# Decode attention's value product one step later than its transposes, in a kernel with merged prompt and decode attention

## The chip, the cores and the metric

The kernel runs on one core of a Trainium2 chip. The metric is the device time of one execution in microseconds (us). The core has five engines that run programs of their own and meet at semaphores: TensorE (PE; its weight loads are listed as PEld), the vector engine (DVE), the scalar engine (ACT), GpSimd (POOL) and SyncE (SP, which here only issues transfers). GpSimd issues transfers too.

## The reference

One inference step of a decoder layer, for a prompt of 1024 tokens and for 8 sequences with 8 new tokens each. Half of the width is gated linear attention, the other half differential attention; output projection, feed-forward and a gated embedding follow. The change is in differential attention, which for the 8 sequences reads a paged cache of 4096 past tokens:

```python
def diff_attend_sample(q, k, v, lam, k_past, v_past):
    ...
    s_past = jnp.einsum('bqhcd,bkhcd->bhcqk', q, k_past).astype(F32) * scale
    s_new = jnp.einsum('bqhcd,bkhcd->bhcqk', q, k).astype(F32) * scale
    s_new = jnp.where(jnp.tril(jnp.ones((T, T), dtype=bool)), s_new, -jnp.inf)
    a = jax.nn.softmax(jnp.concatenate([s_past, s_new], axis=-1), axis=-1)
    w = (a[:, :, 0] - lam * a[:, :, 1]).astype(v.dtype)
    return (jnp.einsum('bhqk,bkhv->bqhv', w[..., :P], v_past)
            + jnp.einsum('bhqk,bkhv->bqhv', w[..., P:], v))
```

A sequence has 32 pages of 128 tokens for the keys and as many for the values, 256 KB a page; 8 sequences make 256 pages of each.

## The kernel before

The kernel is a row of stages. The function `attention` is the third; it works on the prompt's attention and the sequences' attention at once, in one list of `STEPS` = 74 steps, t = 0 to 73, that every engine walks in its own program. The order on each engine is written out by hand; semaphore counts join the engines.

The decode part cuts the cache into groups of 4 pages (512 tokens): `NG` = 8 groups for a sequence, `NKV` = 64 in all. Group t goes through these operations:

- step t: TensorE transposes the keys of the group, one head at a time (`turn_keys`, L1587), into PSUM; ACT copies heads 0 to 2 to SBUF as `dec_kt` (L1470), DVE head 3 (L1751);
- step t + 1: `score` (L1599) multiplies them with the queries;
- step t + 2: DVE takes the maximum (L1756) and copies the scores to `dec_s` (L1762);
- step t + `LAG`, with `LAG` = 9, since the softmax of a sequence needs the maximum over its 8 groups: ACT makes the exponentials (`exps`, L1481), TensorE transposes them (`turn_p`, L1622), DVE copies the transposes to `dec_pt` (`take_p`, L1790, two buffers), and TensorE multiplies them with the values (`values`, L1641), summing a sequence in one PSUM bank.

Once per sequence b there are: `score_new` (L1609) and `take_new` (L1772 to L1778) for the new tokens at t = 8b + 8 and 8b + 9; the exponentials, transpose and copy of their weights (L1486, `turn_new_p` L1616, `take_new_p` L1784) in the step of the sequence's first group (t = 8b + 9); their product with the new values (L1634) ahead of the first value product; `final_scale` (L1796 to L1800); `finalize` (L1807), where DVE scales the finished sum to `dec_osc`; `merge` (L1649), a matmul that adds the two sub-heads; and `copy_os` (L1492) on ACT.

Key transposes, merges, transposed weights and new scores share a ring of three PSUM banks, the class `Ring`. An entry takes the next slot in TensorE's order, and may be filled once the entry three places earlier has been copied out by its owner.

The prompt's units fill the gaps: two steps for a unit, with scores (L1547), exponentials (L1446), their combination (L1728), transposes (L1560), weight copies (L1456), output (L1569) and two output copies (L1462, L1463). The last unit's output stands in step 66. After it DVE normalises the prompt's output in four pieces (`norm_prompt`, L1735).

SyncE loads key pages, GpSimd value pages (L1303). Both rings hold four groups; the loads of value group n wait until the value product of group n - 4 is done:

```python
                else:
                    gp.wait_ge(d["pv_done"], n - VR + 1)
                load_pages(gp, m.table, io["cache_v"], m.vr, n % VR, v_page_in[n % VR], n)
```

After the last load GpSimd scales two tiles of `w_out` (L1428). The next stage begins when all engines have left this one.

Of the kernel before, what the change touches and what calls it, by code (L numbers as in the profile page):

```python
# [1234 lines left out]
NG = NPG // 4  # L1235
NKV = DB * NG
LAG = NG + 1
STEPS = NKV + LAG + 1
UNITS = [(h, i) for h in range(H) for i in (0, 7, 1, 6, 2, 5, 3, 4)]
NU = len(UNITS)  # L1240
HALVES = 2 * NU + 3
# [14 lines left out]
class Ring:  # L1256
# [4 lines left out]
    def __init__(self):  # L1261
        self.index, self.emptied, self.owners = {}, {}, []
        count = {"act": 0, "dve": 0}

        def use(key, owner):
            self.index[key] = len(self.owners)
            count[owner] += 1
            self.emptied[key] = count[owner]
            self.owners.append((owner, count[owner]))

        for t in range(STEPS):
            if t < NKV:
                for h in range(H):
                    use(("keys", t, h), "act" if h < 3 else "dve")
            b, last = divmod(t - LAG - NG, NG)
            if last == 0 and 0 <= b < DB:
                use(("merge", b), "act")
            v = t - LAG
            if 0 <= v < NKV:
                if v % NG == 0:  # L1280
                    use(("new_p", v // NG), "dve")
                use(("p", v), "dve")
            b, last = divmod(t - NG, NG)
            if last == 0 and 0 <= b < DB:
                use(("new_s", b), "dve")
# [33 lines left out]
def attention(nc, io, m, ps, scr, sems):  # L1319
# [57 lines left out]
    with nc.Block() as block:  # L1377
# [53 lines left out]
        @block.scalar  # L1431
        def _(act):
            def prompt_exps(k):

                if not 0 <= k < 2 * NU:
                    return
                n, c = divmod(k, 2)
                i, u = UNITS[n][1], n % 2
                act.wait_ge(s["neg_max"], k + 1)
                if k == 0:  # L1440
                    act.wait_ge(gla_stored, 32)
                    act.wait_ge(d["states_stored"], 32)
                if n >= 2:
                    act.wait_ge(s["turned"], pieces_before(n - 1))
                out = m.ap[:, u, c, 0:2 * shown(i) * P].rearrange("p (b two n) -> p two b n", two=2, n=P)
                act.activation(out, score_view(i).rearrange("p two (b n) -> p two b n", n=P), ACT.Exp, scale=SC,  # L1446
                               bias=neg_p[:, u, c:c + 1], accum_out=sums[:, u, c:c + 1]).then_inc(s["exp_done"], 1)

            def copy_weights(n, q):

                i, u = UNITS[n][1], n % 2
                a, b = 4 * q * P, min(4 * q + 4, i + 1) * P
                act.wait_ge(s["turned"], pieces_before(n) + q + 1)
                if n >= 1:
                    act.wait_ge(s["o_done"], n)
                act.activation(m.wt[:, a:b], W_BANK[:, 0:b - a], ACT.Copy).then_inc(s["wt_copied"], 1)  # L1456

            def copy_out(n):

                (h, i), u = UNITS[n], n % 2  # L1460
                act.wait_ge(s["o_done"], n + 1)
                act.activation(m.a_o[:, i, h * DV:h * DV + DV], W_BANK[:, 0:DV], ACT.Copy, scale=rcp[:, u, 0:1])  # L1462
                act.activation(m.junk[:, :], W_BANK[:, 0:DV], ACT.Square, scale=rcp[:, u, 0:1],  # L1463
                               accum_out=m.a_ss[:, i, h:h + 1]).then_inc(s["o_squared"], 1)

            def take_keys(t, h):
                act.wait_ge(d["ring_filled"], ring.filled(("keys", t, h)))
                if t >= 2:
                    act.wait_ge(d["s_full"], t - 1)
                act.activation(m.kt[:, t % 2, h, :], ring_bank(("keys", t, h)), ACT.Copy).then_inc(d["ring_act"], 1)  # L1470

            def exps(v):
                b, g = divmod(v, NG)
                if g == 0:
                    act.wait_ge(d["negm"], b + 1)
                    if b >= 2:
                        act.wait_ge(d["final"], 4 * (b - 2) + 1)
                act.wait_ge(d["s_taken"], v + 1)
                if v >= 2:
                    act.wait_ge(d["ring_filled"], ring.filled(("p", v - 2)))  # L1480
                act.activation(m.pg[:, v % 2, :], m.ss[:, 512 * g:512 * g + 512], ACT.Exp, scale=SC,  # L1481
                               bias=negm[:, b % 2:b % 2 + 1], accum_out=esum[:, b % 2, g:g + 1]).then_inc(d["exp_done"], 1)
                if g == 0:
                    if b:
                        act.wait_ge(d["ring_filled"], ring.filled(("new_p", b - 1)))
                    act.activation(m.pn[:, 0:NS], m.ss[:, PAST:PAST + NS], ACT.Exp, scale=SC,  # L1486
                                   bias=negm[:, b % 2:b % 2 + 1], accum_out=esum[:, b % 2, NG:NG + 1]
                                   ).then_inc(d["expn_done"], 1)

            def copy_os(b):  # L1490
                act.wait_ge(d["ring_filled"], ring.filled(("merge", b)))
                act.activation(m.os[:, b, :], ring_bank(("merge", b))[0:32, 0:DV], ACT.Copy).then_inc(d["ring_act"], 1)  # L1492

            for t in range(STEPS):
                v = t - LAG
                n, c = divmod(t, 2)
                first_group = 0 <= v < NKV and v % NG == 0
                if 0 <= v < NKV and not first_group:
                    exps(v)
                if t < NKV:  # L1500
                    take_keys(t, 0)
                    take_keys(t, 1)
                if c == 1 and 0 <= n - 1 < NU:
                    copy_weights(n - 1, 0)
                prompt_exps(t - 1)
                if first_group:
                    exps(v)
                if c == 0 and 0 <= n - 2 < NU:
                    copy_out(n - 2)
                if t < NKV:  # L1510
                    take_keys(t, 2)
                if t == 0:
                    act.wait_ge(s["lam_step"], 2)
                    act.activation(m.sc[:, 18:20], m.sc[:, 16:18], ACT.Exp).then_inc(s["lam_step"], 1)
                if c == 1 and 0 <= n - 1 < NU and pieces_of(n - 1) == 2:
                    copy_weights(n - 1, 1)
                if t >= LAG + NG and (t - LAG - NG) % NG == 0:
                    copy_os((t - LAG - NG) // NG)
                if t == HALVES:
                    act.wait_ge(s["o_squared"], NU)  # L1520
                    act.activation(m.a_ss[:, 0:TT - 1, :], m.a_ss[:, 0:TT - 1, :], ACT.Ln, scale=1.0 / DV, bias=m.eps[:, :]
                                   ).then_inc(s["ln_done"], 1)
                    act.wait_ge(s["ln_done"], 1)
                    act.activation(m.a_ss[:, 0:TT - 1, :], m.a_ss[:, 0:TT - 1, :], ACT.Exp, scale=-0.5
                                   ).then_inc(s["rstd_done"], 1)

        @block.tensor
        def _(pe):
# [117 lines left out]
            def merge(b):  # L1646
                pe.wait_ge(d["final"], 4 * b + 4)
                emptied(("merge", b))
                pe.matmul(ring_bank(("merge", b))[0:32, 0:DV], const(m, "merge"), m.osc[:, :], start=True, stop=True  # L1649
                          ).then_inc(d["ring_filled"], 1)  # L1650

            pe.wait_ge(d["zero_done"], 4)
            for t in range(STEPS):
                v = t - LAG
# [8 lines left out]
                if t < NKV:  # L1663
                    turn_keys(t, 2)
                    turn_keys(t, 3)
                if t >= LAG + NG and (t - LAG - NG) % NG == 0:
                    merge((t - LAG - NG) // NG)
                if 0 <= v < NKV:
                    if v % NG == 0:
                        turn_new_p(v // NG)  # L1670
# [5 lines left out]
                    score(t - 1)  # L1676
                if t and t % NG == 0 and t // NG <= DB:
                    score_new(t // NG - 1)
                if 0 <= v < NKV:
                    values(v)  # L1680

        @block.vector
        def _(dve):
# [118 lines left out]
            def finalize(b):  # L1802
                dve.wait_ge(d["final"], b * 4 + 3)
                dve.wait_ge(d["pv_done"], NG * b + NG)
                if b:
                    dve.wait_ge(d["ring_filled"], ring.filled(("merge", b - 1)))
                dve.tensor_scalar(m.osc[:, :], O_BANK[:, 0:DV], cs[:, 1:2], None, ALU.mult).then_inc(d["final"], 1)  # L1807
# [4 lines left out]
            for t in range(STEPS):  # L1812
                v = t - LAG
                n, c = divmod(t, 2)
                if t >= LAG + NG and (t - LAG - NG) % NG == 0:
                    finalize((t - LAG - NG) // NG)
                if 0 <= t - 2 < NKV:
                    max_scores(t - 2)
                if 0 < t - 1 <= NKV and (t - 1) % NG == 0:
# [1325 lines left out]
```

## Time and profile before

| what | value |
|---|---|
| time, median of 3 runs | 1888.35 us (1885.49 to 1888.97) |
| the profiled execution: time, and span in the trace | 1886.4 us, 1884.7 us |
| PE busy in the span | 1775.2 us (94%) |
| DVE, ACT, POOL busy | 1196.6, 736.4, 345.6 us |
| attention stage in the trace | about 432 to 872 us |

Busy time tells what an engine has to do, not that others wait for it. Which of its waits are long, and what ends them, is in the views of waits and in the timeline. A number after a timeline row in brackets is the engine's idle time just ahead of it, and what ended that.

### The profile page before, as it was taken

Reading aid. Unit: us, or ns where it says so; the run is one execution under the profiler, and the core shown is the slowest. Engines: PE = TensorE matmul, PEld = TensorE weight load, DVE = VectorE, ACT = ScalarE, POOL = GpSimd, SP = SyncE. Lnnn points to the kernel's source line nnn. Section 1 sums busy time; section 2 is a strip of 40 time slices with the busy share of each in tenths; the row PEclk is TensorE's granted clock in tenths of the full one; section 3 lists DMA queues with packets and bytes.
Section 4 is the critical chain, followed back from the end, with each engine's and each line's share of the span. In section 5 each row is a group of like instructions: output and inputs, shape, how many; then the busy total and the mean of one; then the engine's idle time right before and its main releaser. Section 6 shows DMA issues by size and latency. Waiting matters only on the chain.

```text
span 1884.7 us, 35480 instructions
## 1 busy us (share of the span) xinstructions
PE 1775.2 (94%) x13062; PEld 1639.1 (87%) x13062; DVE 1196.6 (63%) x1946; ACT 736.4 (39%) x1418; POOL 345.6 (18%) x360
## 2 busy tenths in 40 slices
PE   6999999986999999996999999999999999998998
PEld 6999999984666667665898999999999999998997
DVE  4223642475777777765448877666767888789443
ACT  5113322563556565653224332322232424344420
POOL 1111331001233333332111221121111000000110
PEclk9999999998999999997999999999999999999999
DMA  5323551228999999976011222222222424232121
GB/s 161 107 80 82 141 140 56 72 72 254 323 338 351 349 360 355 351 229 223 28 41 45 92 69 69 80 79 72 69 81 69 157 68 145 74 106 75 57 70 48
DMA packets 232923, 265.73 MB, mean 141 GB/s; under 512 B 16162, under 2 KB 173428, under 8 KB 232756
## 3 DMA queue, kind: packets, MB, share of 16 engines
q1 hardware_dynamic: 211988, 195.36, 33.1%
q0 software_dynamic: 20768, 68.17, 10.6%
q8 instruction: 101, 1.65, 0.4%
q14 instruction: 66, 0.54, 0.1%
HBM read 229.79 MB, written 29.21 MB: 137 GB/s over the span
## 4 chain that ended last, share of the span: by engine, by line
PE 46%; DVE 5%; ACT 1%; issue 1%; DMA 1%; DVEq 0%; ACTq 0%
PE psum L2513 33%; PE psum L150 11%; DVE x_second_lo L2527 1%; DVE unit_lo L1910 1%; DMA x_second_lo_raw<-scratch_z 1%; PE psum L2193 1%; PE psum L2889 0%; ACT unit_hi L1904 0%; DVE rstd_and_products L2571 0%; DVE x_second_lo_raw L2531 0%; DVE h L2571 0%; DVE x_first_lo L2527 0%; ACT x_second_hi L2401 0%; DVE x_lo L2222 0%; DMA x_first_hi_raw<-scratch_z 0%
## 5 line engine op out<-in xcount | busy, mean ns | idle before, releaser
L2513 PE MATMUL psum<-x_second_hi,unit_hi 128*128 128x364 f32 x924 | 304.3, 329 | 8.0 <-DVE x_second_lo L2527 4.8
L2513 PE MATMUL psum<-x_second_lo,unit_hi 128*128 128x364 f32 x924 | 303.1, 328 | 0.0
L2513 PE MATMUL psum<-x_second_hi,unit_lo 128*128 128x364 f32 x924 | 303.1, 328 | 0.0
L1303 POOL DMA_DIRECT2D dec_v<-in_cache_v x256 | 138.0, 539 | 290.3 <-issue 283.8
L150 PE MATMUL psum<-x_hi,w_hi 128*128 128x364 f32 x768 | 182.4, 346 | 9.1 <-DVE x_lo L2222 5.8
L2513 PEld LDWEIGHTS psum<-x_second_hi,unit_hi 128*128 128x128 f32 x924 | 173.7, 188 | 10.9 <-issue 5.6
L2513 PE MATMUL psum<-x_first_hi,unit_hi 128*128 128x364 f32 x528 | 173.7, 329 | 0.4 <-DVE x_first_lo L2527 0.4
L2513 PEld LDWEIGHTS psum<-x_second_hi,unit_lo 128*128 128x128 f32 x924 | 173.7, 188 | 0.0
L2513 PEld LDWEIGHTS psum<-x_second_lo,unit_hi 128*128 128x128 f32 x924 | 173.6, 188 | 0.0
L2513 PE MATMUL psum<-x_first_hi,unit_lo 128*128 128x364 f32 x528 | 173.5, 329 | 0.0
L2513 PE MATMUL psum<-x_first_lo,unit_hi 128*128 128x364 f32 x528 | 173.2, 328 | 0.0
L150 PE MATMUL psum<-x_hi,w_lo 128*128 128x364 f32 x768 | 170.7, 330 | 0.0
L150 PE MATMUL psum<-x_lo,w_hi 128*128 128x364 f32 x768 | 170.0, 330 | 0.0
L1470 ACT ACTIVATE dec_kt<-psum 128x512 f32<-128x512 f32 x192 | 108.7, 599 | 156.1 <-PE psum L1587 156.1
L1904 ACT ACTIVATE unit_hi<-unit_sums 128x512 fp32r<-128x512 f32 (+1 forms) x136 | 83.3, 618 | 217.6 <-PE psum L2513 185.2
L2392 POOL TENSOR_TENSOR w_raw<-w_raw,gains 128x1024 f32<-128x1024 f32 x42 | 90.7, 2160 | 376.2 <-DMA w_raw<-in_w_ffn_gate 208.8
L1587 PE MATMUL psum<-consts,dec_k 128*128 128x128 f32 x1024 | 139.0, 280 | 19.9 <-DMA dec_k<-in_cache_k 8.6
L1904 ACT ACTIVATE unit_hi<-w_raw 128x512 fp32r<-128x512 f32 (+1 forms) x136 | 82.5, 617 | 177.8 <-PE psum L2513 160.5
L1587 PEld LDWEIGHTS psum<-consts,dec_k 128*128 128x128 f32 x1024 | 115.0, 143 | 38.9 <-issue 14.9
L150 PEld LDWEIGHTS psum<-x_hi,w_hi 128*128 128x128 f32 x768 | 131.9, 189 | 18.8 <-DVE x_lo L2222 6.2
L150 PEld LDWEIGHTS psum<-x_hi,w_lo 128*128 128x128 f32 x768 | 134.2, 189 | 0.0
L150 PEld LDWEIGHTS psum<-x_lo,w_hi 128*128 128x128 f32 x768 | 134.0, 189 | 0.0
(313 smaller groups left out, 3321.0 us busy)
## 6 DMA issues: line engine op xcount, KB each, us to landing
dec_k<-in_cache_k SPq DMA_DIRECT2D x256, 256.0 KB, 5.4
dec_v<-in_cache_v POOLq DMA_DIRECT2D x256, 256.0 KB, 5.3
w_raw<-in_w_in SPq DMA_DIRECT2D x25, 512.0 KB, 3.9
scratch_z<-ffn_hidden SPq DMA_DIRECT2D x22, 546.0 KB, 2.8
w_raw<-in_w_ffn_gate SPq DMA_DIRECT2D x22, 512.0 KB, 3.7
w_raw<-in_w_ffn_up SPq DMA_DIRECT2D x22, 512.0 KB, 3.7
w_raw<-in_w_ffn_down SPq DMA_DIRECT2D x16, 512.0 KB, 4.1
feat_swap<-feat_n SPq DMA_DIRECT2D x32, 136.5 KB, 2.4
```

Source lines behind the costliest of these rows:

```text
L150: ins = pe.matmul(out[:, c, 0:SPAN], w(k), x(k)[:, c * SPAN:c * SPAN + SPAN], start=n == 0 and w is whi and x is xhi, stop=n == len(ks) - ...
L1303: eng.dma_start(ring[:, slot, p:p + 1, :], cache[bass.ds(page, 1)].rearrange("o t f -> t o f")).then_inc(sem, 16)
L1470: act.activation(m.kt[:, t % 2, h, :], ring_bank(("keys", t, h)), ACT.Copy).then_inc(d["ring_act"], 1)
L1587: ins = pe.transpose(ring_bank(key)[:, p * P:p * P + P], m.kr[:, t % KR, p, h * P:h * P + P], ident)
L1904: act.activation(m.uhi[unit][:, 0:half_tiles(t), :], unit_source(m, t, unit), ACT.Copy).then_inc(s["w_hi"], 1)
L1910: dve.tensor_tensor(m.ulo[unit][:, 0:n, :], unit_source(m, t, unit), f32(m.uhi[unit][:, 0:n, :]), ALU.subtract).then_inc(s["w_lo"], 1)
L2193: ins = pe.transpose(misc[n % 2][:, (j - a) * P:(j - a) * P + rows], m.xr[0:rows, j, k * P:k * P + P], ident[0:rows, 0:rows])
L2392: gp.tensor_tensor(m.raw[:, u], m.raw[:, u], gain(m, "ffn").unsqueeze(2).broadcast_to([P, KT, P]), ALU.mult).then_inc(s["w_scaled"], 1)
L2513: ins = pe.matmul(bank[b], w[unit][:, j, :], x[slot][:, j, :], start=start and j == 0 and w is m.uhi and x is m.xhi7, stop=j == k - 1 and ...
L2527: dve.tensor_tensor(m.xlo7[slot][:, 0:n, :], source, f32(m.xhi7[slot][:, 0:n, :]), ALU.subtract).then_inc(s["x_lo"], 1)
```

## The change

The value product of group v is issued by TensorE one step later (`VLAG` = `LAG` + 1), behind the next group's `turn_p`. `finalize`, `merge` and `copy_os` of a sequence follow by one step, and so does their place in the ring. Exponentials, transposes, the copies to `dec_pt` and `final_scale` keep their steps. There are 75 steps instead of 74. Below the added line all line numbers are one higher (L1641 is L1642 in the changed kernel).

```diff
 LAG = NG + 1
-STEPS = NKV + LAG + 1
+VLAG = LAG + 1
+STEPS = NKV + VLAG + 1
...
-            b, last = divmod(t - LAG - NG, NG)
+            b, last = divmod(t - VLAG - NG, NG)
             if last == 0 and 0 <= b < DB:
                 use(("merge", b), "act")
...
-                if t >= LAG + NG and (t - LAG - NG) % NG == 0:
-                    copy_os((t - LAG - NG) // NG)
+                if t >= VLAG + NG and (t - VLAG - NG) % NG == 0:
+                    copy_os((t - VLAG - NG) // NG)
...
-                if t >= LAG + NG and (t - LAG - NG) % NG == 0:
-                    merge((t - LAG - NG) // NG)
+                if t >= VLAG + NG and (t - VLAG - NG) % NG == 0:
+                    merge((t - VLAG - NG) // NG)
                 if 0 <= v < NKV:
                     if v % NG == 0:
                         turn_new_p(v // NG)
...
-                if 0 <= v < NKV:
-                    values(v)
+                if 0 <= t - VLAG < NKV:
+                    values(t - VLAG)
...
-                if t >= LAG + NG and (t - LAG - NG) % NG == 0:
-                    finalize((t - LAG - NG) // NG)
+                if t >= VLAG + NG and (t - VLAG - NG) % NG == 0:
+                    finalize((t - VLAG - NG) // NG)
```

TensorE in the step of a sequence's first group and the step after it (in the kernel before; the rows begin with the third and fourth key transposes):

```order
L1587 MATMUL psum<-consts,dec_k 128x128 x8
L1649 MATMUL psum<-dec_osc,consts 32x128
L1616 MATMUL psum<-consts,dec_pn 128x128
L1622 MATMUL psum<-consts,dec_p 128x128 x4
L1560 MATMUL psum<-consts,att_p 128x128
L1547 MATMUL psum<-att_k_101,att_q 128x128 x2
L1599 MATMUL psum<-dec_kt,dec_qb 32x512 x4
L1634 MATMUL psum<-dec_new_v,dec_ptn 32x128 x4
L1641 MATMUL psum<-dec_v,dec_pt 32x128 x16
L1587 MATMUL psum<-consts,dec_k 128x128 x8
L1569 MATMUL psum<-att_v,att_wt 128x128 x5
L1587 MATMUL psum<-consts,dec_k 128x128 x8
```

The same place in the changed kernel, up to the second step's transposes of weights:

```order
L1588 MATMUL psum<-consts,dec_k 128x128 x8
L1617 MATMUL psum<-consts,dec_pn 128x128
L1623 MATMUL psum<-consts,dec_p 128x128 x4
L1561 MATMUL psum<-consts,att_p 128x128
L1548 MATMUL psum<-att_k_101,att_q 128x128 x2
L1600 MATMUL psum<-dec_kt,dec_qb 32x512 x4
L1642 MATMUL psum<-dec_v,dec_pt 32x128 x16
L1588 MATMUL psum<-consts,dec_k 128x128 x8
L1570 MATMUL psum<-att_v,att_wt 128x128 x5
L1588 MATMUL psum<-consts,dec_k 128x128 x8
L1650 MATMUL psum<-dec_osc,consts 32x128
L1623 MATMUL psum<-consts,dec_p 128x128 x4
```

The merge (L1649, now L1650) has moved from ahead of the new weights' transpose to ahead of the next step's weight transposes, and the product with the new values (L1634) has left the first step; the value product that stands there now is that of the group before.

The vector engine around the same place (in the kernel before; the first two rows are the prompt's, the next three `final_scale`):

```order
L1713 TENSOR_REDUCE att_small<-psum 128x1
L1715 TENSOR_SCALAR att_small<-att_small 128x1
L1796 TENSOR_REDUCE att_small<-att_small 128x1
L1798 RECIPROCAL att_small<-att_small 128x1
L1800 TENSOR_TENSOR att_small<-att_small 128x1
L1807 TENSOR_SCALAR dec_osc<-psum,att_small 128x128
L1756 TENSOR_REDUCE att_small<-psum 128x1
L1772 TENSOR_TENSOR dec_s<-psum,consts 128x64
```

The same place in the changed kernel:

```order
L1714 TENSOR_REDUCE att_small<-psum 128x1
L1716 TENSOR_SCALAR att_small<-att_small 128x1
L1797 TENSOR_REDUCE att_small<-att_small 128x1
L1799 RECIPROCAL att_small<-att_small 128x1
L1801 TENSOR_TENSOR att_small<-att_small 128x1
L1757 TENSOR_REDUCE att_small<-psum 128x1
L1773 TENSOR_TENSOR dec_s<-psum,consts 128x64
```

`finalize` (L1807) has left the place ahead of the maximum; in the changed kernel it stands ahead of the next step's maximum.

## Rows read from the trace of the kernel before

**Rows 1.** Stretches: us, busy of PE, PEld, DVE, ACT, POOL (instructions), clock, DMA.

```profile
700.00:740.00 40.00, 38.90 (x494) 28.81 (x492) 31.27 (x66) 23.92 (x61) 14.55 (x27) 1.00 1.04 368
```

**Rows 2.** Waits of PE, 500 to 820 us: waiter, releaser, us, times, longest.

```profile
PE psum L1547 <- ACT att_p L1446: 7.6, 19, 0.6
PE psum L1616 <- ACT dec_kt L1470: 5.8, 6, 1.0
PE psum L1587 <- DVE dec_s L1772: 5.7, 6, 1.0
```

**Rows 3.** Tile dec_pt, 500 to 838 us: idle time before it, us and times.

```profile
  issue: 19.5, 65
  DVE dec_pt L1790: 5.7, 19
```

**Rows 4.** Waits of PE, 838 to 872 us.

```profile
PE psum L1641 <- DVE dec_pt L1790: 6.5, 7, 2.3
```

**Rows 5.** Timeline of PE (start, us): steps 7 and 10, score and next keys.

```profile
479.32 1.06 PE L1599 MATMUL psum<-dec_kt,dec_qb 128*32 128x512 f32 x8
480.31 0.87 PE L1587 MATMUL psum<-consts,dec_k 128*128 128x128 f32 x6
...
499.58 1.06 PE L1599 MATMUL psum<-dec_kt,dec_qb 128*32 128x512 f32 x8
...
501.45 0.77 PE L1587 MATMUL psum<-consts,dec_k 128*128 128x128 f32 x5
```

**Rows 6.** Timeline, a step with a sequence's first group, one of six.

```profile
739.41 0.35 DVE L1807 TENSOR_SCALAR dec_osc<-psum,att_small 128x128 f32<-128x128 f32 x1
739.68 0.68 DVE L1756 TENSOR_REDUCE att_small<-psum 128x1 f32<-128x512 f32 x1
...
740.55 1.09 PE L1587 MATMUL psum<-consts,dec_k 128*128 128x128 f32 x8 [0.92 <-DVE dec_s L1772]
...
741.16 0.72 ACT L1481 ACTIVATE dec_p<-dec_s,att_small 128x512 f32<-128x512 f32 x1 [0.34 <-DVE att_small L1778]
...
742.22 0.57 ACT L1470 ACTIVATE dec_kt<-psum 128x512 f32<-128x512 f32 x1
...
742.93 0.30 PE L1616 MATMUL psum<-consts,dec_pn 128*128 128x128 f32 x1 [0.96 <-ACT dec_kt L1470]
...
743.07 0.61 PE L1622 MATMUL psum<-consts,dec_p 128*128 128x128 f32 x4
```

**Rows 7.** Timeline, the step after it (the same pair in all six).

```profile
749.09 0.60 ACT L1470 ACTIVATE dec_kt<-psum 128x512 f32<-128x512 f32 x1
749.15 0.60 PE L1622 MATMUL psum<-consts,dec_p 128*128 128x128 f32 x4
```

**Rows 8.** Timeline of PE and DVE, steps 63 to 72.

```profile
831.64 1.06 PE L1641 MATMUL psum<-dec_v,dec_pt 128*32 128x128 f32 x32
...
842.76 2.42 PE L1569 MATMUL psum<-att_v,att_wt 128*128 128x128 f32 x10
...
854.88 1.68 PE L1641 MATMUL psum<-dec_v,dec_pt 128*32 128x128 f32 x32 [1.91 <-DMA dec_v<-in_cache_v]
...
862.01 4.76 DVE L1735 TENSOR_TENSOR att_o<-att_o,att_o_ss 128x1024 f32<-128x1024 f32 x1
862.14 1.93 PE L1641 MATMUL psum<-dec_v,dec_pt 128*32 128x128 f32 x32 [0.78 <-DVE dec_pt L1790]
...
867.43 1.08 PE L1641 MATMUL psum<-dec_v,dec_pt 128*32 128x128 f32 x32 [2.31 <-DVE dec_pt L1790]
```

**Rows 9.** Timeline of POOL, 826 to 870 us: loads of value pages.

```profile
833.94 0.54 POOL L1303 DMA_DIRECT2D dec_v<-in_cache_v  x1 [1.94 <-issue]
...
844.07 0.54 POOL L1303 DMA_DIRECT2D dec_v<-in_cache_v  x1 [1.26 <-issue]
...
861.37 0.54 POOL L1303 DMA_DIRECT2D dec_v<-in_cache_v  x1 [0.61 <-issue]
```

**Rows 10.** Line L1303 on POOL, 826 to 866 us: from issue to landing.

```profile
DMA to landing us min/median/max: 2.8/3.7/7.2
```

**Rows 11.** Stretch after the batch at 538 us, columns as in rows 1.

```profile
541.00:545.00 4.00, 3.97 (x30) 2.23 (x34) 2.00 (x6) 1.13 (x4) 0.49 (x1) 0.57 1.04 337
```

## The prediction

> **What bounds the kernel now.** I read first the table of stretches, to see whether TensorE, the vector engine or the transfers fill the attention stage (432 to 872 us). In a middle stretch of 40 us TensorE is busy 38.90 us at the full granted clock, the vector engine 31.27, the scalar engine 23.92 [rows 1]. The DMA engines also show a share of 1.04 there, so I looked for TensorE waiting for a transfer: in the list of its waits between 500 and 820 us there is none. That list has three entries, 19.1 us together [rows 2]: prompt scores behind the scalar engine's exponentials (7.6 us), and two waits that come once per sequence, the transpose of the new weights behind a `dec_kt` copy (5.8 us, 6 times) and the key transposes behind `dec_s` (5.7 us, 6 times). The wait that the change takes away, value product behind the `dec_pt` copy, is not in it. The view of the tile says why: the weight loads stood 0.30 us before a value product in 19 places put down to the copy (5.7 / 19), and 0.30 us in 65 places where nothing was waited for (19.5 / 65) [rows 3]. The copy is done by then; the 0.30 us is there with or without it. So steps 10 to 63 are bound by TensorE's own order, and only the tail (steps 65 to 73, no keys left) shows real waits for the copy: 6.5 us in 7 places [rows 4].
>
> **The change part by part.** Times are of the profiled execution.
>
> *The wait removed, dense steps.* 0 us, by [rows 2, 3]. It cannot be negative: the product uses a copy made a step earlier, and `values(v-2)`, which frees the buffer of `take_p(v)`, now stands at the end of the step before, while that copy comes late in its step.
>
> *One value product fewer in the dense steps.* The first product leaves step 9, the last comes one step later, where TensorE is not full. What a product costs in line: from a decode score to the next key transposes 1.87 us with it (499.58 to 501.45), 0.99 without (479.32 to 480.31) [rows 5]. The difference is 0.88; step 9 ran partly at a lower clock, so up to twice that. I take -1.0 us, bounds -0.9 and -1.8.
>
> *The step with a first group (t = 17, 25, ... 57, six of them in the dense part).* Before, the vector engine does `finalize` (L1807) ahead of the maximum (L1756) and of `take_new`, for which TensorE's third and fourth key transposes wait (0.92 us at 740.55). The start of L1756 follows that of L1807 by 0.27 us (739.41, 739.68), so the wait gets 0.27 shorter; the scalar engine, idle 0.34 us for the same chain, follows by as much. TensorE meets that engine again at L1616 and L1622. Before, `merge` stood in the ring of three PSUM slots between keys and new weights, so the new weights wanted the slot of the third keys: L1616 began at 742.93, after the `dec_kt` copy (742.22 + 0.57 = 742.79), and L1622 at 743.07 [rows 6]. After, the new weights take the slot of the second keys, and it is `turn_p` that wants the third's: 742.79 - 0.27 + 0.14 = 742.66. Gain 0.4 us. The merge itself was free here: it ran inside this wait.
>
> *The step after it (t = 18, 26, ... 58).* `merge` now stands behind the key transposes, and `turn_p` therefore takes the slot that the third keys of the same step hold (in other steps, that of the second). The scalar engine empties it late, after the prompt's two output copies: L1470 from 749.09 to 749.69, while L1622 began at 749.15 [rows 7]. With the 0.14 us of the rows above, 749.82: 0.67 us later. The merge's matmul hides in that wait. The copy for the vector engine, the prompt scores, the decode score and the value product of this step stand behind `turn_p` and all shift with it. `finalize` now heads the vector engine's row of this step and waits for the end of the step before, but its next customer there (L1762 for the score) has over a microsecond to spare, so I price it at 0; if not, 0.35 us. `copy_os` lands where the scalar engine is ahead of TensorE. Net per sequence 0.67 - 0.40 = +0.27; six times, +1.6 us. Bounds: if the slot is empty in time, only the gain stays (6 x -0.40 = -2.4); if the gain doesn't come, 6 x 0.67 = +4.0.
>
> *The tail.* GpSimd issues the loads of values one page at a time, and the load of group n waits for the product of group n - 4. In the tail it issues without a pause: 844.07 to 861.37 for 15 pitches, 1.153 us each, 4.6 us per group [rows 9]. Before, the product of step 63 (group 54) ends at 831.64 + 1.06 = 832.70 [rows 8], and 1.24 us later, at 833.94, comes the first page of group 58. After, the same step holds the product of group 53, so this moment starts group 57: 28 pages are left to issue instead of 24. The last issue moves from 861.37 to 833.94 + 27 x 1.153 = 865.1, plus the +0.6 us that front and batches leave (-1.0 + 1.6) = 865.7. From issue to landing a page takes 3.7 us in the median, 2.8 to 7.2 [rows 10]; the last page is there at 869.4. In the kernel before it is there about 865.1, but the last product begins only at 867.43, waiting 2.31 us for `dec_pt`, because the copy stood behind a normalisation of 4.76 us on the vector engine [rows 8], which ran beside GpSimd's scaling of `w_out`. In the changed kernel that copy needs only the product of group 61, one or two loads earlier, so the transfer alone decides. Start of the last product: 869.4 instead of 867.43, **+2.0 us for everything up to there**. After it the chain is the same (product, `finalize`, `merge`, copy, store). Two things may add: the load of group 60 also waits for the product of group 56, which now stands behind the prompt's last output (842.76 + 2.42 [rows 8]) and may come up to 1.2 us after GpSimd is free; and the last product may run at the lower clock (1.93 instead of 1.08 us). So the tail alone is +1.4, bounds +0.5 (landing after 2.8) and +3.5.
>
> The page DMA: Bandwidth & Descriptors of the Trainium skill (Anatomy of one DMA, SWDGE path) fits a GpSimd DMA as 2.0 us plus its bytes over 436e3 per us, an estimate of 2.6 us for 256 KB; by it the last page lands 1.1 us earlier and the sum would be +0.9. The trace shows more than the page, and the sum stays with the trace.
>
> **Sum.** -1.0 + 1.6 + 1.4 = +2.0 us on 1886.4 us, the profiled execution: 1888.4. The runs' median is 1888.35, 1.95 above that execution; on its scale I forecast 1890.4 us, +0.1%. About 0.2% (3.8 us) is what a measurement of this kernel can tell from no change.
>
> **The rivals.**
> *A: the tail is TensorE's.* If the loads came in time, the 6.5 us of waits for the copy [rows 4] would go, for one more step of 1.7 us (0.61 for the transposes [rows 6], 1.08 for the product [rows 8]): -4.8, and with the +0.6 in front -4.2, so 1882.2, or 1884.1 on the median's scale. For it speaks that these waits are plain in the trace; against it that the product at 854.88 already waits for `dec_v` [rows 8] and that GpSimd has no gap after 844.07. 10%.
> *B: `turn_p` is not held in the step after.* If the scalar engine reaches the third copy earlier than the rows say, the batches bring -2.4 instead of +1.6: sum -2.0, 1886.4 on the median's scale, still no change. Against it: the copy follows the prompt's output copies, which follow TensorE, in every one of the six steps. 15%.
> *C: the array's clock, slower.* After the waits at 538 to 541 us the granted clock fell to 0.57 for 4 us [rows 11], mostly the lower level (1.2 GHz), which cost 0.43 x 4 = 1.7 us; the other five batches of the dense part kept 2.4 GHz. The change spreads TensorE's idle time over two steps of each batch. If two more batches drop, the sum is +5.4 (1893.8); with four, +8.8 (1897.2). It decides from two on. Against it: the idle time per batch stays about what it was (0.92 + 0.96 before, about 0.65 + 0.7 + 0.4 after). 25%, together with tail and batches both at their upper ends. The Trainium skill's TensorE: Matmul & The Clock Gate (Part 1) says that an idle array falls back to half its clock and activity releases it; by that rule the drops could also go, as the one at 541 us (-1.7).
>
> **How the numbers follow.** Forecast (+0.5 to +3.7) 50%, A 10%, B 15%, C 25%. A lies beyond 0.2% on the fast side, and a B that meets a vanished clock drop adds a little: faster 0.11. C gives most of slower: 0.24. The rest, same: 0.65. The range leaves half of A and the far end of C outside: 1885.5 to 1896.0.
>
> **What would show it.** Right: no wait for `dec_pt` at the value product anywhere but perhaps the very end; L1623 (`turn_p`) waiting some 0.4 to 0.7 us for `dec_kt` in the six steps after a first group; the `dec_s` wait near 0.65 us instead of 0.92; GpSimd issuing without a gap from about 834 us to 865 us, and the products of groups 60 to 63 waiting for `dec_v` some 4.6 us apart. Wrong: an attention stage that ends before 870 us (A or B), or stretches of half clock after more than one batch (C).

## The result and the profile after

| | before | after |
|---|---|---|
| median | 1887.96 us (1884.01 to 1891.45, 20 runs) | 1891.29 us (1887.36 to 1899.13, 20 runs) |
| ratio | 1 | 1.0021 (95% interval 1.0014 to 1.0028) |
| span of the profiled execution | 1884.7 us | 1889.9 us |

The kernel is slower, by 3.3 us in the medians and by 0.0021 x 1888 = +4.0 us in the ratio. The forecast was +2.0 us (1890.4); its range held the time.

The waits of TensorE between 500 and 820 us in the changed kernel answer to [rows 2]: waiter, releaser, us, times, longest.

```profile
PE psum L1548 <- ACT att_p L1447: 7.5, 19, 0.6
PE psum L1617 <- ACT dec_pn L1487: 4.5, 6, 0.8
PE psum L1588 <- DVE dec_s L1773: 3.5, 6, 0.6
PE psum L1623 <- ACT dec_kt L1471: 2.5, 12, 0.3
```

The wait for `dec_s` fell from 5.7 to 3.5 us, that of the new weights from 5.8 to 4.5 (it is now their exponentials, L1487, that end it), and `turn_p` (L1623) waits for the third key copy, 12 times now. In the view of the tile `dec_pt` (500 to 838 us; idle time before it, us and times) nothing was won:

```profile
  issue: 20.2, 65
...
  DVE dec_pt L1791: 5.1, 17
```

The idle time of 0.30 us ahead of a value product is still there ([rows 3]: 0.30 us each; now 5.1 / 17 = 0.30 and 20.2 / 65 = 0.31), though the copy is a whole step older. It was no wait.

The step of a sequence's first group and the one after it, in the timeline of the changed kernel, answer to [rows 6, 7] (the first three rows are one step, the last three the next; both lie at the full granted clock):

```profile
688.04 1.09 PE L1588 MATMUL psum<-consts,dec_k 128*128 128x128 f32 x8 [0.62 <-DVE dec_s L1773]
...
689.90 0.33 PE L1617 MATMUL psum<-consts,dec_pn 128*128 128x128 f32 x1 [0.77 <-ACT dec_pn L1487]
...
690.48 0.63 PE L1623 MATMUL psum<-consts,dec_p 128*128 128x128 f32 x4 [0.25 <-ACT dec_kt L1471]
...
696.36 1.04 PE L1588 MATMUL psum<-consts,dec_k 128*128 128x128 f32 x8
697.33 0.41 PE L1650 MATMUL psum<-dec_osc,consts 128*32 128x128 f32 x2
697.91 0.63 PE L1623 MATMUL psum<-consts,dec_p 128*128 128x128 f32 x4 [0.17 <-ACT dec_kt L1471]
```

The kernel before has in the second step the row below, and then `turn_p` at 749.15 [rows 7]:

```profile
748.28 1.04 PE L1587 MATMUL psum<-consts,dec_k 128*128 128x128 f32 x8
```

From the last key transposes to `turn_p` it is 0.87 us there (748.28 to 749.15) and 1.55 in the changed kernel (696.36 to 697.91): 0.68 us more. The merge (0.41 us) stands in it, and `turn_p` waits for the third key copy, which shows as 0.17 us of idle time. In the first step the same distance shrinks from 2.52 us (740.55 to 743.07 in [rows 6]) to 2.44, behind a `dec_s` wait that is 0.37 us shorter in the mean of six.

What both steps make together is read from the distance between the new tokens' scores (`score_new`), which come once in 8 steps. In the changed kernel:

```profile
486.08 0.29 PE L1610 MATMUL psum<-dec_new_k,dec_qb 128*32 128x64 f32 x8
533.88 0.29 PE L1610 MATMUL psum<-dec_new_k,dec_qb 128*32 128x64 f32 x8
...
634.46 0.29 PE L1610 MATMUL psum<-dec_new_k,dec_qb 128*32 128x64 f32 x8
684.79 0.29 PE L1610 MATMUL psum<-dec_new_k,dec_qb 128*32 128x64 f32 x8
735.03 0.29 PE L1610 MATMUL psum<-dec_new_k,dec_qb 128*32 128x64 f32 x8
```

and in another execution of the kernel before (run e8 below):

```profile
488.62 0.29 PE L1609 MATMUL psum<-dec_new_k,dec_qb 128*32 128x64 f32 x8
537.29 0.29 PE L1609 MATMUL psum<-dec_new_k,dec_qb 128*32 128x64 f32 x8
...
639.00 0.29 PE L1609 MATMUL psum<-dec_new_k,dec_qb 128*32 128x64 f32 x8
689.14 0.29 PE L1609 MATMUL psum<-dec_new_k,dec_qb 128*32 128x64 f32 x8
739.13 0.29 PE L1609 MATMUL psum<-dec_new_k,dec_qb 128*32 128x64 f32 x8
```

The first distance holds step 9, which lost its value product: 48.67 before, 47.80 after. Two later ones: 50.14 and 49.99 before, 50.33 and 50.24 after. In most executions one or two of the seven distances are about 1.5 us longer, from a stretch at the granted clock of 0.5. With each distance taken from an execution without one (of the same dense order: e5 has that of before), the seven are before 48.67 + 50.22 + 49.99 + 50.14 + 50.00 + 50.15 + 47.87 = 347.04 us, after 47.80 + 50.34 + 50.24 + 50.33 + 50.24 + 50.33 + 48.13 = 347.41. **The dense part costs +0.4 us.** The rest is behind it.

TensorE's value products in the tail of the changed kernel, which answer to [rows 8]:

```profile
854.57 1.94 PE L1642 MATMUL psum<-dec_v,dec_pt 128*32 128x128 f32 x32 [4.58 <-DMA dec_v<-in_cache_v]
857.48 1.93 PE L1642 MATMUL psum<-dec_v,dec_pt 128*32 128x128 f32 x32
860.31 1.08 PE L1642 MATMUL psum<-dec_v,dec_pt 128*32 128x128 f32 x32
864.60 1.08 PE L1642 MATMUL psum<-dec_v,dec_pt 128*32 128x128 f32 x32 [2.62 <-DMA dec_v<-in_cache_v]
869.07 1.93 PE L1642 MATMUL psum<-dec_v,dec_pt 128*32 128x128 f32 x32 [3.39 <-DMA dec_v<-in_cache_v]
```

and GpSimd's issues (answering to [rows 9]; from 843.63 on the pitch is 1.15 us without a gap):

```profile
833.97 0.54 POOL L1304 DMA_DIRECT2D dec_v<-in_cache_v  x1 [1.94 <-issue]
...
843.63 0.54 POOL L1304 DMA_DIRECT2D dec_v<-in_cache_v  x1 [0.79 <-issue]
...
865.43 0.54 POOL L1304 DMA_DIRECT2D dec_v<-in_cache_v  x1 [0.60 <-issue]
```

No product of the tail waits for its copy any more ([rows 4]: 6.5 us); instead 4.58 + 2.62 + 3.39 = 10.6 us go by for transfers (before: the 1.91 us at 854.88 in [rows 8]). The five products are those of groups 59 to 63: only 59, 62 and 63 wait, while 60 and 61 follow at the pace of TensorE at half clock. From the eighth `score_new` (835.03 before, 835.07 after) to the last issue it is 26.3 us before and 30.4 after, and to the next stage's first copy (`w_hi`) 36.86 and 39.31 us. That copy and the first matmul of the next stage's main loop (on `x_again`), before and after:

```profile
871.89 1.06 ACT L2115 ACTIVATE w_hi<-w_raw 128x1024 fp32r<-128x1024 f32 x1 [1.92 <-PEq L1377]
...
898.56 1.03 PE L2193 MATMUL psum<-consts,x_again 128*128 128x128 f32 x8
```

```profile
874.38 1.06 ACT L2116 ACTIVATE w_hi<-w_raw 128x1024 fp32r<-128x1024 f32 x1 [1.92 <-PEq L1378]
...
902.86 1.03 PE L2194 MATMUL psum<-consts,x_again 128*128 128x128 f32 x8
```

The next stage then starts slower: between these two rows it takes 26.67 us before and 28.48 after. Stretches of 5 us (columns as in [rows 1]), in the kernel before and in the changed one:

```profile
875.00:880.00 5.00, 4.29 (x17) 3.98 (x17) 4.97 (x8) 2.60 (x4) 0.00 (x0) 0.59 0.93 342
880.00:885.00 5.00, 3.03 (x21) 2.77 (x21) 2.97 (x6) 2.59 (x6) 0.00 (x0) 1.00 1.02 413
```

```profile
880.00:885.00 5.00, 4.25 (x18) 3.77 (x17) 4.08 (x8) 1.91 (x5) 0.00 (x0) 0.50 1.01 399
885.00:890.00 5.00, 4.02 (x22) 3.71 (x22) 2.11 (x4) 1.35 (x3) 0.00 (x0) 0.75 1.05 353
```

Both stages begin at 0.50 (1.2 GHz), and TensorE's idle time just ahead of the first matmul is the same 5.79 us in both. By these shares the clock is back at 1.00 at about 879.1 before, 3.6 us behind the first matmul (875.47), and at about 887.5 after, 9.5 us behind it (877.95).

### The profile page after: what moved, and what is told of

Same layout as the page of the kernel before. It is cut to its first block, busy times and chain, and to the rows that moved or that the text cites. A ratio compares the mean times of both kernels' runs of the same rounds, so it can differ in the third digit from the quotient of the medians.

```text
span 1889.9 us, 35480 instructions
## 1 busy us (share of the span) xinstructions
PE 1779.3 (94%) x13062; PEld 1641.2 (87%) x13062; DVE 1192.7 (63%) x1946; ACT 735.8 (39%) x1418; POOL 342.3 (18%) x360
## 4 chain that ended last, share of the span: by engine, by line
PE 47%; DVE 5%; ACT 1%; issue 1%; DVEq 0%; ACTq 0%
PE psum L2514 34%; PE psum L150 12%; DVE x_second_lo L2528 1%; DVE unit_lo L1911 1%; PE psum L2194 1%; PE psum L2890 0%; DVE rstd_and_products L2572 0%; DVE x_second_lo_raw L2532 0%; DVE h L2572 0%; DVE x_first_lo L2528 0%; ACT unit_hi L1905 0%; DVE x_lo L2223 0%; PE psum L2047 0%; DVE h_lo L2022 0%; DVE unit_sums L1925 0%
```

## The experiments

**e4 and e8: both kernels again, unchanged.**

> The changed kernel once more, unchanged, for what differs from one execution to the next. T: the wait for dec_v of the products in the tail and the six batches (+0.25 us each on eight steps) come back to within 0.1 us; the places of half clock in the dense part (one in the first trace, two in the kernel before) may be others. The 1.8 us lost at the start of the next stage comes back if it follows from the end of the tail (TensorE idle there), and doesn't if it was chance. Time 3 to 4 us over the kernel before.

> The kernel before once more, unchanged, for the spread of its profile: batches 50.0 to 50.2 us apart except where the clock drops, tail 32.4 us from the last score_new to the last product, 26.7 us from the next stage's first copy to its first transposes of x. If the 1.8 us of the changed kernel at that place are chance, some execution of this one may show them too. Time within 1.5 us of the kernel before.

The changed kernel gave 1891.87 us (11 runs), ratio 1.0021 (1.0012 to 1.0031); the kernel before 1888.68 (11 runs), 1.0005 (0.9995 to 1.0014). So 0.2% is the change's and not the execution's. In e4 the three waits for pages come back in their sum (4.25 + 3.36 + 2.77 = 10.4 us) but not one by one; 0.1 us was expected. The new profile of the kernel before corrects something that my forecast rested on. Its last group, from the timeline of all engines (the first row is a piece of the prompt's normalisation, the second GpSimd's scaling of `w_out`):

```profile
863.82 1.22 DVE L1735 TENSOR_TENSOR att_o<-att_o,att_o_ss 128x1024 f32<-128x1024 f32 x1
...
863.99 4.66 POOL L1428 TENSOR_TENSOR w_raw<-w_raw,small 128x1024 f32<-128x1024 f32 x2
...
867.48 1.88 PE L1641 MATMUL psum<-dec_v,dec_pt 128*32 128x128 f32 x32 [1.84 <-DMA dec_v<-in_cache_v]
```

In the profile that I had read GpSimd's scaling had begun first:

```profile
861.92 3.76 POOL L1428 TENSOR_TENSOR w_raw<-w_raw,small 128x1024 f32<-128x1024 f32 x2
```

The normalisation of 4.76 us in [rows 8] takes 1.22 in e8, and the last product waits for its pages, not for the copy. It starts 30.34 us after the eighth `score_new` (837.14); in the profile that I had read it was 32.40, in the changed kernel 34.00 and (e4) 33.82. Behind it, though, e8 needs 5.45 us to `w_hi` and that profile 4.46, so that up to there the difference is 36.86 against 35.79 us.

**e11: the kernel before without that collision.**

```diff
+            gp.wait_ge(s["normed"], H)
             gp.wait_ge(gain_set, 2)
```

> The kernel before, with one wait added: GpSimd scales w_out only after the vector engine has done all four pieces of the prompt's normalisation, so that the two never run side by side. In the profiled execution of before the last piece took 4.76 us beside that scaling, in another execution 1.22. If my forecast took a saving from a collision that is there in some executions only, the last value product starts some 30.3 us after the last score of new tokens in this kernel's profile, as in the execution without a collision (32.4 with it), no product waits over 1 us for its copy, and the median is 0 to 2 us under the kernel before. If the collision costs nothing that the loads would not cost anyway, the median stays within 0.5 us.

1886.66 us (12 runs), before beside it 1886.36 (21 runs), ratio 0.9998 (0.9989 to 1.0008). All four normalisations take 1.22 us and the last product starts 30.87 us after the eighth `score_new` (836.05), waiting for pages:

```profile
866.92 1.08 PE L1642 MATMUL psum<-dec_v,dec_pt 128*32 128x128 f32 x32 [1.79 <-DMA dec_v<-in_cache_v]
```

The median does not move. The interval (-2.1 to +1.5 us) is wider than what the collision costs, so this doesn't show how often the kernel before pays it; but up to `w_hi` the tail is 36.60 us here, hardly less than the 36.86 with the collision.

**e5: the later product in the last sequence only.**

```diff
+LATE = NKV - NG
+def sums_at(b):
+    return LAG + NG + NG * b + (b == DB - 1)
...
-                if 0 <= t - VLAG < NKV:
-                    values(t - VLAG)
+                if 0 <= v < LATE:
+                    values(v)
+                elif LATE <= v - 1 < NKV:
+                    values(v - 1)
```

(`finalize`, `merge`, `copy_os` and the ring follow `sums_at`.)

> The kernel before, with the later value product for the last sequence alone (groups 56 to 63; no product in step 65; finalize, merge and copy_os of the last sequence one step later). Theory T: the dense part is that of the kernel before (eight steps in 50.0 to 50.2 us, no wait of turn_p for the third keys), and the tail alone is paid for: the load of group 60 waits for the product of group 56, one step later, so the last product starts 1 to 2 us later than in the kernel before, counted from the last score_new (32.4 there, 34.0 in the changed kernel). Time +1 to +2 us on the kernel before. Rival (the tail gains by the waits for dec_pt that go): 2 to 4 us faster.

1890.38 us (11 runs), ratio 1.0015 (1.0005 to 1.0024). The dense part is that of before (50.22, 50.00, ... 50.00, 50.13; the one left out holds a half-clock stretch), the tail that of the changed kernel: 39.01 us, next stage 28.43. Its last products in the timeline:

```profile
862.01 1.60 PE L1648 MATMUL psum<-dec_v,dec_pt 128*32 128x128 f32 x32 [2.93 <-DMA dec_v<-in_cache_v]
...
866.35 1.94 PE L1648 MATMUL psum<-dec_v,dec_pt 128*32 128x128 f32 x32 [1.69 <-DMA dec_v<-in_cache_v]
871.39 1.93 PE L1648 MATMUL psum<-dec_v,dec_pt 128*32 128x128 f32 x32 [3.10 <-DMA dec_v<-in_cache_v]
```

By the trace the loss is in the last eight groups and what follows them; the batches are the small part. (The time alone doesn't divide them: the interval reaches from 1 to 4.5 us.)

**e3: the merge behind `turn_p`, in the code and in the ring.**

```diff
-                if t >= VLAG + NG and (t - VLAG - NG) % NG == 0:
-                    merge((t - VLAG - NG) // NG)
                 if 0 <= v < NKV:
                     if v % NG == 0:
                         turn_new_p(v // NG)
                     turn_p(v)
+                if t >= VLAG + NG and (t - VLAG - NG) % NG == 0:
+                    merge((t - VLAG - NG) // NG)
```

> The changed kernel, with merge moved behind turn_p in TensorE's order and in the ring. T (the step after a first group is late since merge makes turn_p take the slot of the third keys): the waits of L1623 for dec_kt in these steps go, eight steps take about 0.4 us less than in the changed kernel (50.25 to 49.85), six times; 2 to 2.5 us less in all, 1 to 2 us over the kernel before. Rival: if another wait holds that step, its length stays within 0.1 us of 50.25 and the total that of the changed kernel. The tail stays as it is (last product near 867 to 869 us).

1888.84 us (11 runs), ratio 1.0009 (1.0000 to 1.0017). The waits between 500 and 820 us keep the entry for the third keys in six places only:

```profile
PE psum L1623 <- ACT dec_kt L1471: 1.5, 6, 0.3
```

and 8 steps take 50.00 and 50.10 us: 0.24 less than in the changed kernel, where 0.4 was expected. So the merge ahead of `turn_p`, with the wait that it brings, costs about 0.24 x 6 = 1.4 us. The tail stays long, at 39.65 us; the next stage's start was 26.60 in this execution.

**e1 and e2: value groups 58, 60 and 62 loaded by SyncE**, in the changed kernel and in the kernel before.

```diff
+            for n in SP_VALUES:
+                sp.wait_ge(d["pv_done"], n - VR + 1)
+                load_pages(sp, m.table, io["cache_v"], m.vr, n % VR, sp_v_in[n], n)
             sp.wait_ge(s["o_done"], NU)
...
+                if n in SP_VALUES:
+                    continue
```

> The changed kernel, with the value pages of groups 58, 60 and 62 loaded by SyncE instead of GpSimd (same gates, own semaphores; the load of w_out stands behind them on SyncE). Theory T (the tail is bound by GpSimd's issue of one page in 1.15 us, gated one step later): two issuers halve that, the waits of the products of groups 60 to 63 for dec_v shrink, the last product begins near 861 us of the trace instead of 869.07, and the kernel gains 5 to 8 us on the changed one, so 1.5 to 4.5 us under the kernel before. Rival R (the tail is bound by TensorE, its copies or its clock, and the loads only fit in): within 1 us of the changed kernel, 3 to 4 us over the kernel before.

> The kernel before, with the same three groups loaded by SyncE. T: here the copy in the same step paces the tail once loads come in time (2.45 us a step), the wait for dec_v at 854.88 goes, and the last product begins near 861 to 863 us instead of 867.43: 4 to 6 us faster than the kernel before. The two kernels with two loaders then lie within 2 us of each other. R: no gain for the kernel before (under 1 us), since the copies bound its tail.

Changed: 1887.78 us (12 runs), 1.0004 (0.9995 to 1.0012). Before: 1886.20 (11 runs), 0.9997 (0.9988 to 1.0006). With a second loader the changed kernel loses its 0.2% against before, as it should if GpSimd's row of issues sets the tail; but 5 us or more were expected and 3.5 came. The timeline of e1 shows what was next:

```profile
858.45 0.54 POOL L1305 DMA_DIRECT2D dec_v<-in_cache_v  x1 [0.61 <-issue]
...
865.67 1.25 PE L1652 MATMUL psum<-dec_v,dec_pt 128*32 128x128 f32 x32 [3.73 <-DMA dec_v<-in_cache_v]
```

The last page is issued 7.0 us earlier than in the changed kernel and the last product begins 3.4 us earlier: 7.2 us go by from its issue to the product that waits for it, while the 1 MB of `w_out` is under way, which SyncE issues at 854.81 here and at 844.08 in the changed kernel. The kernel before gains nothing, where 4 to 6 us were expected: six products there still wait 0.7 us each for the copy of their own step, and from 859.7 us on its granted clock is 0.50.

**e6 and e7: `w_out` loaded earlier as well** (ahead of group 60); e6 on the changed kernel with the merge of e3, e7 on the kernel before.

```diff
+            for n in SP_VALUES:
+                if n == SP_VALUES[1]:
+                    sp.wait_ge(s["o_done"], NU)
...
```

> The changed kernel with three edits: merge behind turn_p, groups 58, 60 and 62 loaded by SyncE, and w_out loaded as soon as the prompt is done, ahead of group 60. In the first run with two loaders the last pages took 7.2 us to land, beside the 1 MB of w_out, and the last product waited for them until 865.67. T: with w_out out of the way they take about 3.7 us, the last product starts near 862 us (28 us after the last score_new), and the kernel takes 4 to 6 us less than that run, about 4 to 5 us under the kernel before. Rival (the collision isn't the cause): last product where it was, gain only 1.4 us from merge.

> The kernel before with groups 58, 60 and 62 loaded by SyncE and w_out loaded ahead of group 60. T: here the copy within the step paces the tail (2.45 us a step); the last product starts near 28 to 29 us after the last score_new instead of 32.4, and the kernel takes 2 to 4 us less than before. Against e6 it shows what the later value product is worth once the loads come in time: 1 to 2 us in favour of the changed order. Rival: no difference between the two, as the loads still decide both.

Both missed: e6 1886.94 us (11 runs), 1.0001 (0.9992 to 1.0010), e7 1891.21 (11 runs), 1.0017 (1.0005 to 1.0028). In e6 `w_out` is issued at 846.01, about where the changed kernel has it, and the pages of group 59 land late; GpSimd has a hole of 3.71 us, and the scaling meets the last normalisation:

```profile
855.56 1.63 PE L1653 MATMUL psum<-dec_v,dec_pt 128*32 128x128 f32 x32 [3.89 <-DMA dec_v<-in_cache_v]
...
858.41 0.54 POOL L1305 DMA_DIRECT2D dec_v<-in_cache_v  x1 [3.71 <-issue]
...
862.42 3.76 POOL L1437 TENSOR_TENSOR w_raw<-w_raw,small 128x1024 f32<-128x1024 f32 x2
...
864.44 2.83 DVE L1747 TENSOR_TENSOR att_o<-att_o,att_o_ss 128x1024 f32<-128x1024 f32 x1
```

In e7 the loads are done early (last issue 858.14), and behind a wait of 4.56 us for pages at 858.61 every product waits for its copy:

```profile
862.37 1.94 PE L1652 MATMUL psum<-dec_v,dec_pt 128*32 128x128 f32 x32 [0.79 <-DVE dec_pt L1801]
...
866.14 1.94 PE L1652 MATMUL psum<-dec_v,dec_pt 128*32 128x128 f32 x32 [0.78 <-DVE dec_pt L1801]
...
869.91 1.94 PE L1652 MATMUL psum<-dec_v,dec_pt 128*32 128x128 f32 x32 [0.79 <-DVE dec_pt L1801]
```

A product every 3.77 us, at 1.2 GHz; at 2.4 GHz the same order gives one every 2.45 us (e11: 861.00 to 863.46). From the eighth `score_new` to the last product e7 takes 33.80 us, e6 30.98, though its last issue comes 24.9 us after that score and that of e7 22.0. These 2.8 us speak for the later product where loads are out of the way, as rival A has it; but the clock has a part in them that no run takes out: it stays at 0.50 to the end in e7 and is back at 1.00 at 866 us in e6. And e6 as a whole is no faster than the kernel before.

**e9 and e10: extra transposes on TensorE in the tail**, whose results nobody reads, in the changed kernel and in the kernel before.

```diff
+            def fill(count):
+                pe.wait_ge(s["o_squared"], NU)
+                for k in range(count):
+                    pe.transpose(W_BANK[:, 0:P], ident, ident)
...
+                if t >= NKV + 5:
+                    fill(8)
...
+            fill(16)
```

> The changed kernel with extra work on TensorE alone, whose results nobody reads: eight transposes ahead of the value product in steps 69 to 74, where TensorE otherwise waits for the loads, and sixteen after the last merge. If the lower granted clock explains the part of the tail that I had not in my sum (last value product 1.93 us instead of 1.08, next stage's start 28.4 us instead of 26.6), the last product runs in 1.08 us, the next stage's start takes 26.7 us or less, and the kernel is 2 to 3 us under the changed one, that is 0 to 2 us over the kernel before. If the loads alone set the tail and the lower clock follows from something else, the extra work moves nothing (0.2 per cent slower than before, as the changed kernel), or costs its own 1 to 2 us at the end.

> The kernel before with the same extra work in steps 69 to 73 and after the last merge. If the clock counts there too (its next stage starts with matmuls of 1.11 us that take 0.66 later), the stage's start takes 25 us instead of 26.7 and the kernel is 1 to 3 us faster than before. If not, it is the same, or up to 2 us slower by the extra work ahead of a product that already has its operands.

e9: 1892.46 us (8 runs), 1.0032 (1.0020 to 1.0044); e10: 1887.68 (11 runs), 1.0001 (0.9990 to 1.0012). Neither gained. In e9 the last product still ran at half clock, and so did the first of the transposes behind the last merge (the clock is back at 1.00 at 873.6 us):

```profile
867.43 1.93 PE L1642 MATMUL psum<-dec_v,dec_pt 128*32 128x128 f32 x32 [2.27 <-DMA dec_v<-in_cache_v]
...
870.45 4.49 PE L1656 MATMUL psum<-consts 128*128 128x128 f32 x24
```

They ended at 874.94 and held the end of the stage: from the last product to `w_hi` 7.79 us instead of 5.31. The next stage's start took 26.67 us in e9, but it did so in some executions without extra work too, so this test leaves the role of the clock open. In e10 the last five products all ran in 1.08 us and the granted clock was 1.00 until 875.6 us; yet at the first matmul of the next stage (876.89) it was 0.50 again, its start took 26.67 us instead of the 25 expected, and the time did not move.

**e12: not what its name says.**

> The changed kernel with a ring of five groups of values instead of four, so that a load waits for the product five groups earlier and comes free at the same step as in the kernel before. If the later release of the buffers is what the tail pays, GpSimd's last issue comes some 26.3 us after the last score of new tokens (before 26.3, changed 30.4), the last product some 30 us after it (changed 34.0), and the kernel is 4 to 6 us under the changed one, 1 to 3 us under the kernel before (rival A of the prediction, in which the tail is TensorE's). If the tail is held by something else, TensorE's own order or the lower clock, it stays 34 us and the kernel stays 0.2 per cent over before.

What ran is the changed kernel as it is, with four groups. So the expectation is untested (no run has a ring of five) and the run is one more timing of the changed kernel: 1891.47 us (10 runs) beside 1886.36 (21 runs), ratio 1.0025 (1.0015 to 1.0035). Its profile has a tail of 39.01 us and a next stage's start of 26.67.

## Why the prediction was nearly right, point by point

- *The wait removed: 0.* Right: the 0.30 us ahead of a product stayed, and in the list of TensorE's waits in the changed kernel (432 to 880 us) no value product waits for its copy.
- *One product fewer in the dense steps: -1.0.* Measured 48.67 to 47.80: -0.87.
- *First-group step and the step after it: +0.27 per sequence, +1.6.* Right in its mechanism, and e3 shows it. In the second step `turn_p` came 0.68 us later (forecast 0.67); in the first it gained 0.37 by the shorter `dec_s` wait and 0.08 behind it (forecast 0.27 and 0.14). The net was +0.12 to +0.26 per distance, together 347.41 - 347.04 + 0.87 = +1.24. The idle time that shows ahead of `turn_p` is 0.17 us and not the 0.4 to 0.7 that I had named as a sign: the merge fills the rest, as the working had said it would.
- *The tail: +1.4.* The mechanism was right in each part (buffers released a step later, a nearly unbroken row of issues, 865.43 for the last against a forecast of 865.7, last product 869.07 against 869.4), and e5 alone brings most of the loss. Only the products of groups 62 and 63 then waited for their pages, not all from 60 on. **The size was off.** Up to `w_hi` the tail is 36.86, 35.79 and 36.60 us (before, e8, e11) against 39.31, 39.26 and 39.01 (after, e4, e12): 39.2 - 36.4 = +2.8 instead of +1.4. How the missing 1.4 divides is not settled. In the two profiles of the forecast the last product starts 1.6 us later, nearly as forecast, and runs 0.85 us longer at 1.2 GHz, the addition that I had named and left out. But the start of 867.43, from which I counted, held the collision of the normalisation with GpSimd's scaling. In e8, e10 and e11 the normalisation is not held up, and the last product starts 1.5 to 2.4 us earlier after the eighth `score_new`; in e8 and e11 1.0 to 1.3 us of that are lost again behind it.
- *What was not in the sum: the next stage.* Where the granted clock stays at 0.50 for more than 9 us after work resumes, its start takes 28.4 us instead of 26.7: in the profiles of after, e4 and e5, not in e3, e9 and e12, and in none with the tail order of before. Taken by its share in these six, half of 1.8 is an estimate of +0.9. Why it happens is open: the idle time just ahead of the first matmul is 5.79 us in before, after and e12 alike, and e12 is the same program as after.
- *The sum.* +0.4 + 2.8 + 0.9 = +4.1 us, against ratios of 1.0021, 1.0021 and 1.0025, that is +4.0 to +4.7 us. Forecast: +2.0, with +0.5 to +3.7 as the bounds of its own mechanism. The ratio lies just above these (on the scale of the medians they end at 1892.05, and 1891.29 lies just inside). What is missing from the forecast lies in the tail and behind it, not in the dense part.
- *Rival A* failed for the reason given: the loads do not come in time. *Rival B* too: `turn_p` is held. *Rival C* is not borne out where it was placed: seven executions with before's dense order show 7 long distances, seven with the changed one 6. What the clock cost beyond that lies at the tail's end and in the next stage.

## What to carry to other kernels

Before a consumer is moved later, list what its completion releases: here a buffer, and behind it a serial row of 1.15 us issues that in the tail passes the whole step on to the end. A saving that rests on a collision seen in one execution should be set at zero until a second execution, or the order of the two instructions, shows that it must happen. And where a wait disappears, read the idle time in places where nothing was waited for: if it is the same 0.30 us, there was no wait.

## What was not expected of the hardware

- In these traces the vector engine's `TENSOR_TENSOR` and GpSimd's don't share time, they exclude each other. In before GpSimd began 0.09 us earlier (861.92), and the normalisation ended 1.09 us after GpSimd's two instructions (862.01 + 4.76 against 861.92 + 3.76). In e6 it ended 1.09 us after them too (2.83 us long), and in e7 (1.31 us). In e8 the vector engine began 0.17 us earlier: 1.22 us for it, 4.66 instead of 3.76 for GpSimd, which ended 3.61 us after the vector engine. A shift of 0.26 us in the starts thus decides over 3.5 us. The Trainium skill, SBUF — State Buffer (SBUF: two separate sides), says that the port pair the two have in common is locked for a whole instruction by whoever comes first and the other blocks; all four cases agree, and in before the vector engine waited for both of GpSimd's instructions.
- From issue to landing a page of 256 KB took 3.4 to 3.7 us in the median in the tails of before, after, e11 and e12, but up to 7.7 us; in e1 a late one was the last, and the product that waited for it began 7.2 us after its issue.
- The half-clock stretches between the first and the last `score_new` cost some 1.5 us each and differ between executions of one program: the two profiles of the kernel before both have one some 6 us after the second `score_new` (at 541 and 543 us), only one has another near 490 us; e2 and e9 have none at all.
